# Two of four groups of the inverse products moved into the state chain, on four 64x64 tiles of the array

## What is computed

```python
def step(S, inp):
    rt, wt, kt, vt, at, bt = inp
    sa = jnp.einsum('dbhvk,dbhk->dbhv', S, at)
    S = S * wt[..., None, :] + sa[..., :, None] * bt[..., None, :] + vt[..., :, None] * kt[..., None, :]
    y = jnp.einsum('dbhvk,dbhk->dbhv', S, rt) if emit else None
    return S, y
```

## Time and profile before

| what | value |
|---|---|
| median of 3 runs | 2757.31 us (2756.01 to 2758.84) |
| the profiled execution, own time | 2753.63 us |
| its span | 2751.8 us |
| PE busy | 2687.9 us (98%) |
| DVE busy | 1404.5 us (51%) |
| ACT busy | 734.9 us (27%) |
| mean granted PE clock | 0.996 |

### The profile page before, as it was taken

How to read it: one execution, slowest core, us unless ns; L and a number is a source line. 1 busy time by engine, 2 the same in 40 slices (tenths; PEclk the granted TensorE clock), 3 DMA queues, 4 the chain that set the end, 5 groups by cost and what they waited for, 6 DMA issues and landing times.

```text
span 2751.8 us, 61051 instructions
## 1 busy us (share of the span) xinstructions
PE 2687.9 (98%) x26901; PEld 1731.7 (63%) x26901; DVE 1404.5 (51%) x2723; ACT 734.9 (27%) x1502; POOL 215.1 (8%) x184
## 2 busy tenths in 40 slices
PE   7999999999999999999999999999999999999999
PEld 3455555556444445748888444666666677788887
DVE  2676666674322233337778212677777633314541
ACT  3234333432222221111111002433443322211110
POOL 1000000000000002215444000000000000000000
PEclk9999999999999999999999999999999999999999
DMA  7111111111333333344543224222221234346554
GB/s 266 55 51 43 51 43 51 51 41 43 107 100 105 97 112 92 92 131 148 154 129 107 71 76 141 61 59 59 59 59 51 58 109 111 110 139 191 153 148 121
DMA packets 500007, 264.52 MB, mean 96 GB/s; under 512 B 42864, under 2 KB 493888, under 8 KB 499232
## 3 DMA queue, kind: packets, MB, share of 16 engines
q1 hardware_dynamic: 498016, 251.58, 31.7%
q0 software_dynamic: 1728, 9.03, 0.9%
HBM read 255.33 MB, written 5.24 MB: 95 GB/s over the span
## 4 chain that ended last, share of the span: by engine, by line
PE 91%; ACT 5%; DVE 2%; issue 1%; DMA 1%; SPq 0%; ACTq 0%; DVEq 0%
PE psum L515 34%; PE psum L517 14%; PE psum L1181 12%; PE psum L1293 8%; PE psum L781 2%; PE psum L549 2%; PE psum L1014 1%; PE psum L890 1%; PE psum L1002 1%; PE psum L590 1%; PE psum L992 1%; PE psum L758 1%; PE psum L731 1%; PE psum L771 1%; PE psum L904 1%
## 5 line engine op out<-in xcount | busy, mean ns | idle before, releaser
L515 PE MATMUL psum<-hT,strips 128*128 128x256 f32 (+1 forms) x2252 | 706.4, 464 | 0.8 <-issue 0.8
L515 PEld LDWEIGHTS psum<-hT,strips 128*128 128x128 f32 x2252 | 418.7, 191 | 228.4 <-issue 191.7
L517 PE MATMUL psum<-hT,strips 128*64 128x512 f32 (+1 forms) x1896 | 393.5, 535 | 2.1 <-DVE arena L2372 1.4
L1293 PE MATMUL psum<-arena,strips 128*128 128x512 f32 (+1 forms) x704 | 227.6, 486 | 0.6 <-DVE arena L2811 0.6
L1293 PEld LDWEIGHTS psum<-arena,strips 128*128 128x128 f32 x704 | 133.7, 190 | 93.1 <-issue 83.2
L517 PEld LDWEIGHTS psum<-hT,strips 128*64 128x64 f32 x1896 | 116.5, 136 | 108.0 <-issue 84.5
L515 PE MATMUL psum<-arena,strips 128*128 128x256 f32 (+1 forms) x416 | 125.9, 461 | 0.9 <-DVE done L2660 0.9
L2811 DVE SCALAR_TENSOR_TENSOR arena<-psum,mod,arena 128x256 f32<-128x256 f32 x24 | 10.9, 481 | 193.7 <-PE psum L1293 193.7
L515 PEld LDWEIGHTS psum<-arena,strips 128*128 128x128 f32 x416 | 78.9, 190 | 45.0 <-issue 36.8
L2193 DVE TENSOR_SCALAR arena<-arena 128x512 f32<-128x512 f32 (+1 forms) x88 | 70.0, 795 | 70.1 <-ACT arena L2045 68.0
L1181 PE MATMUL psum<-arena,rwkv_branch 128*128 128x256 f32 x424 | 99.0, 379 | 0.0
(11 more groups left out here) (303 smaller groups left out, 4169.0 us busy)
## 6 DMA issues: line engine op xcount, KB each, us to landing
strips<-in_w_in_dram SPq DMA_DIRECT2D x152, 512.0 KB, 3.8
strips<-in_ada_w_dram SPq DMA_DIRECT2D x80, 512.0 KB, 4.9
strips<-in_ffn_up_dram SPq DMA_DIRECT2D x46, 512.0 KB, 3.8
strips<-in_ffn_down_dram SPq DMA_DIRECT2D x32, 512.0 KB, 3.8
conv_branch<-in_ffn_up_dram SPq DMA_DIRECT2D x28, 512.0 KB, 4.9
arena<-in_ada_w_dram SPq DMA_DIRECT2D x4, 2048.0 KB, 15.9
strips<-in_w_in_dram SPq DMA_DIRECT2D x32, 256.0 KB, 3.3
strips<-in_a_out_w_dram SPq DMA_DIRECT2D x16, 512.0 KB, 3.8
```

The source lines that it names most:

```text
L515: return pe.matmul(o, lhs, rhs, start=start, stop=stop, skip_group_check=True)
L517: ins = pe.matmul(o[64 * h:64 * h + 64], lhs[:, 64 * h:64 * h + 64], rhs, start=start, stop=stop, skip_group_check=True)
L1293: ins = mm(s.o[:, lo:T], strip[:, b, j, :], hid[:, k, lo:T], k == 0, k == FT - 1)
```

## The change

`through_inverse` is called three times for a group: once ahead of the chain for m = 0 and 1, once behind `state_in(1)` for m = 2, and once behind `state_in(2)` for m = 3. The late two go into a Q buffer instead of an A buffer. There the products of row half p write bank p, and head h = 1 writes the other half of the partitions, so that the four (p, h) fall on four different 64x64 tiles; ACT copies them out with four copies of half the length. The dense steps between m = 1 and m = 2 in layer 0 go; instead 4 units (layer 0) or 3 (layer 1) follow m = 1, halved; the hops are a little smaller. `diagonal_blocks(i + 1)` moves ahead of the last hop. In layer 1 the pair products of the context chunks (64 columns) are issued as two 64x64 products each. On ACT `values(0)` or, in layer 0, `conv_gate(i + 1)` goes ahead of the late copies. On DVE `keys(0)` is one chunk earlier in the last group of layer 0. SP waits until ada units 0 and 1 have landed before it issues units 2 and 3.

```diff
@@ pair_products
                     for c in range(4 * j, 4 * j + 4):
-                        for h in range(2):
+                        for e in range(2 if n == CH else 0):
+                            for h in range(2):
+                                ins = one(PS[rows(e), b0 + h, (c % 4) * n:(c % 4 + 1) * n], BK[d][rows(h), c, e, :],
+                                         ar[d][rows(h), c, 0, :])
+                        for h in range(2 if n == P else 0):
                             ins = one(PS[:, b0 + h, (c % 4) * n:(c % 4 + 1) * n],
@@ through_inverse on PE
-                def through_inverse(i, ahead, steps):
-
-                    for j in range(2):
-                        pe.wait_ge(*slots[f"v{j}", l, i].freed)
-                    pe.wait_ge(*slots["t10", l, i].freed)
-                    sv = take(Q, "mv", l, i)
-                    for m in range(4):
-                        if m == 2 and ahead and wide:
-                            fill(steps, 2)
-                        s = take(A, f"lrb{m}", l, i)
+                def through_inverse(i, ahead, first):
+
+                    if first == 0:
+                        for j in range(2):
+                            pe.wait_ge(*slots[f"v{j}", l, i].freed)
+                        pe.wait_ge(*slots["t10", l, i].freed)
+                        sv = take(Q, "mv", l, i)
+                    for m in range(2) if first == 0 else (first,):
+                        s = take(A if m < 2 else Q, f"lrb{m}", l, i)
...
-                                ins = one(PS[r, BANK_A[s.b], q * n:(q + 1) * n].rearrange("p (k t) -> p k t", t=CH),
+                                to = rows(p if m < 2 or h == 0 else 1 - p)
+                                bank = BANK_A[s.b] if m < 2 else BANK_P[s.b] + p
+                                ins = one(PS[to, bank, q * n:(q + 1) * n].rearrange("p (k t) -> p k t", t=CH),
@@ the group on PE
-                    through_inverse(i, ahead, steps)
-                    hop = (3.4 if ahead else 4) if wide else 2 if ahead else 2.3
+                    through_inverse(i, ahead, 0)
+                    halved[0] = True
+                    fill(steps, 4 if wide else 3)
+                    hop = (3.3 if ahead else 4) if wide else 1.8 if ahead else 2.1
                     for c in range(NCH):
                         state_in(c, i)
-                        halved[0] = True
+                        if c in (1, 2):
+                            through_inverse(i, ahead, c + 1)
                         if c == NCH - 1:
                             outputs_of_states(i)
+                            if ahead:
+                                diagonal_blocks(i + 1)
                         if c > 0:
                             fill(steps, hop)
                         if c < NCH - 1:
                             state_out(c, i)
                             fill(steps, hop)
-                    if ahead:
-                        diagonal_blocks(i + 1)
                     fill(steps, everything)
@@ SP
                     if l == 0 and c == COL_W:
+                        for u in range(2):
+                            sp.wait_ge(adab.full[u], 16)
                         load_unit(512)
                         load_unit(D + 512)
@@ ACT
-                def through_inverse(i):
-                    for m in range(4):
+                def through_inverse(i, m0, m1):
+                    for m in range(m0, m1):
                         s = filled(f"lrb{m}", i)
+                        if m > 1:
+                            for p in range(2):
+                                o = PS[:, BANK_P[s.b] + p, :].rearrange("p (d h k t) -> p d h k t", d=2, h=2, k=2)
+                                for h in range(2):
+                                    r, at_ = (slice(64 * x, 64 * x + 64) for x in (p, p if h == 0 else 1 - p))
+                                    ins = act.copy(EE[r, 1:3, 1, :, h, 2 * (m % 2) + p].rearrange("p k d t -> p d k t"),
+                                                   o[at_, :, h])
+                            ins.then_inc(s.free, 1)
+                            continue
...
-                    through_inverse(i)
+                    through_inverse(i, 0, 2)
+                    if not ahead:
+                        values(0)
+                    elif lo == 0:
+                        conv_gate(i + 1)
+                    through_inverse(i, 2, 4)
                     if ahead:
-                        if lo == 0:
-                            conv_gate(i + 1)
                         conv_centre(i + 1)
...
                     else:
-                        values(0)
                         values(1)
@@ DVE
-                        if not ahead and c == (4 if lo else 3):
+                        if not ahead and c == (4 if lo else 2):
                             keys(0)
```

More of the change, by code:

```diff
@@ L1782, in through_inverse @@
                         ins.then_inc(s.free, 1)
-                        if m < 2:
-                            value_products(m, i)
+                        value_products(m, i)
                 def conv_gate(i):
```

## The result

| | kernel before | changed kernel |
|---|---|---|
| median | 2758.06 us (2756.01 to 2758.84, 4 runs) | 2731.23 us (2729.31 to 2734.66, 4 runs) |
| profiled execution, own time | 2753.63 us | 2730.94 us |
| its span | 2751.8 us | 2729.1 us |

The ratio is 0.9903, with a 95% interval of 0.9892 to 0.9915: faster by 1.0%, or 22.7 us between the two profiled executions, where I had written 21.8. By the medians it is 26.8 us here, and 24.3 us when both kernels were measured again (first experiment). The total hides misses of opposite sign, so here is where PE stands in the two traces, read as the start of the same product in each.

A forecast was written before the change was run, and what follows sets the result against it. PE, busy 2687.9 of 2751.8 us, was taken as the bound. Layer 0 (-6.9, last group -2.0), layer 1 (-9.6, last -2.3) and start (-1.0) sum to -21.8 us: 2731.8 profiled, 2735.5 median; range 2724 to 2750.

The forecast's parts named there:

- The late products: `through_inverse`, m = 2 and 3: 70 to 35 ns a record on four tiles; -1.13 us (layer 0), -1.46 (layer 1) a group.
- first rival: Late products: the four tiles don't overlap, 70 ns a record stays, +4 us, 2761; chance 0.10.
- Switches: Changes of tile shape on PE, some 0.1 us each: -0.15 and -0.1 us a group in layer 0, -0.1 in layer 1.
- the +0.1 that never came: Layer 0's chain at chunks 1 and 4, fitting by under 0.1 us: +0.1 us in each of 7 groups.
- Stalls in the hops: PE waits on DVE: `gated` +0.3 us in layer 0; before `state_out(3)` and `state_in(6)` +1.05 in layer 1, each of 7 groups.
- the rival by which they do not show (2726): Hops: extra cover lets DVE catch up, waits stay under 0.2 us a group, -9 us; chance 0.17.
- the one by which layer 1's chain absorbs the gain (2749): Layer 1: each of 7 groups stalls 2 us more because DVE is nearly full, +14 us; chance 0.10.
- The pair products: Layer 1's context chunks: 32 split records take 0.56 us at 17.5 ns each; -0.86 us in each of 8 groups.
- The last group of layer 0: The 1.1 us wait for `keys(0)` goes, the second V strip waits 0.2 more: -0.9 us, -2.0 with late products.
- The start: The second ada unit lands earlier, as units 2 and 3 no longer share the DMA engines: -1.0 us of 0 to 1.7.
- the other side: ACT's late copies are slower than taken and hold the chain through 32 waits: +20 us, 2777; chance 0.05.
- The rest of layer 1: Layer 1's 8 chains: -1.37 us in each of 7 groups, -2.3 in the last, -11.9 in all.

The follow-up runs named there:

- first experiment: The changed kernel unedited, measured again beside the kernel before: 2732.07 us, ratio 0.9912, against 2756.32 us.
- two-tile run: Changed kernel with the late products still in the chain, but both heads writing the partitions of their own row half: 2745.03 us, ratio 0.9959.
- run with the earlier frees: Changed kernel with `gated` and `keys(1)` one chunk earlier on DVE and layer 1's hop 2 instead of 1.8: 2722.22 us, ratio 0.9876.
- run ahead of the chain: Changed kernel with the four-tile late products and ACT's copies issued right behind the early ones: 2775.81 us, ratio 1.007.
- doubled products: Layer 1's first-group context pair products whole, issued twice: 2731.58 us in the changed kernel (split kept in other groups), 2755.55 us in the kernel before.

## Why the prediction was right, and where it was not

**The late products** were the main term and right. I took 0.56 us for 16 records and the trace has 0.55; 70 ns a record became 34. The two-tile run holds the other half of it: 13 us is what four tiles give over two, so the first rival (the tiles don't overlap, 2761) is out. In layer 1 the late products mix with `state_in` in the trace; at 0.55 us each as in layer 0 they cost 1.43 us less a group (1.01 work, 0.42 waits), forecast 1.46.

**Switches** were mis-sized. A layer 0 group went from 74.71 to 73.23 us, -1.48 instead of -0.98. The late products follow `state_in` in the same tile shape, and each time `state_in` costs 0.17 instead of 0.27 us, and about as much less in layer 1 (0.82 us with the late products, where 0.37 and 0.55 would be 0.92): -0.2 a group in both layers, a term that my own 0.1 us a switch would have given had I applied it there. With the dense steps (-0.3, forecast -0.25) and the +0.1 that never came, this is most of the 3 us of layer 0.

**Stalls in the hops** were right, each in place and nearly in size: 0.60 us of waiting for `gated` (forecast 0.6, up from 0.37 instead of 0.33), 0.53 before `state_out(3)` (0.6), 0.28 before `state_in(6)` (0.4). The run with the earlier frees took them away and gained 9.9 us, so the rival by which they do not show (2726) is out, and so is the one by which layer 1's chain absorbs the gain (2749): there are no waits in chunks 3 to 7 beyond these two.

**The pair products** gave 0.60 us a group, forecast 0.86. A split set costs 0.69 us (1745.20 to 1746.15, less the wait of 0.26), 22 ns a record, not 17.5; and the next piece then waits 0.26 us for DVE (L2498), so 0.34 is left. My row of 11 ns (128 records of 32 columns on sixteenths) was too kind a guide. The rule in the page "TensorEngine Tiling (Array Packing)" of the Trainium skill, section Instruction Overhead, about 60 cycles a product, gave an estimate of 25 ns and 0.8 us for a set; the trace lies between it and me, a little nearer to it. The page says of up to 60 columns that they take the same time, not of every size, as I had put it; these products have 64. By its own work the split gives under 3 us; the rest of what the run without it lost is the first group's gaps and clock, less what the later groups' gaps gave back.

**The last group of layer 0** is a step that failed. I wrote that its 1.1 us wait "should go with its earlier place", naming `keys(0)`. It did not go; it grew from 1.10 to 2.03 us, since what PE needs there is the buffer that `keys(1)` frees at c = 5, and PE now gets there sooner. -0.9 forecast, +0.9 measured. Moving `keys(1)` took it away. The group as a whole still gained 1.7 us of the 2.0 forecast, since its late products with their waits went from 2.96 (670.75 to 673.71) to 1.10 us.

**The start** is the other step that failed: 0 instead of -1.0 us. I had the second unit land earlier because units 2 and 3 no longer share the DMA engines with it. Its products do start 0.95 us earlier (22.72 after, 23.67 in the earlier trace rows), but 0.93 of that is there before PE uses any unit (the wait for x ends at 9.99 instead of 10.91); the wait for the unit is 1.64 us instead of 1.70. New is a wait of 1.6 us for a strip, and the first `half_step` waits for DVE, 3.1 us instead of 2.5. I took only PE's waits for the unit and not what ends last behind them.

The pair of traces is kind to the edit, too: the first `half_step` starts at 120.93 before and at 120.97 after, but at 121.0 to 124.8 us (mean 123.1) in the nine traces with SP's wait, and at 120.2 to 121.4 (mean 120.9) in the five without it. All nine have a wait of 1.2 to 2.9 us for that strip, four of the five without have at most 0.5 (the fifth 1.9); and in the five that start at 123.8 or later the granted clock falls to 0.50 behind it, near 39 us (this row and window are the changed kernel's, measured again):

```profile
39.19 2.53 PE L549 MATMUL psum<-hT,strips 128*128 128x512 f32 x3 [2.59 <-DMA strips<-in_w_in_dram]
```

```profile
39.50:43.00 3.50, 3.50 (x5) 0.51 1.05 365
```

So by the traces the wait costs some 2 us at that point rather than giving 1; the medians of the two runs without it are too close to confirm or deny that.

**ACT** (the other side, 2777) held nothing up: 1.50 us against my 1.46. The run ahead of the chain shows that this rival was not idle talk, since there PE's waits for ACT are 30.8 us.

**The first group of layer 1** was in no term but for its pair products, and is worth 7.3 us of the 22.7: most of it a gap of 3.61 us and the half clock behind it. The doubled products show that these do not hang on work or tiles, and the packets tie them to blocks of instructions. Without this group I was 6 us too optimistic. The rest of layer 1 gave 6.9 instead of 11.9: a group without "issue" gaps gained 1.1 instead of 1.37 us, and the next six groups together only 4.1. Their "issue" gaps did not shrink (8.3 us before, 8.4 after, at other pieces and up to 3.9 us a group), and behind one of 1.62 us that ends at 1980.90 the changed kernel runs at half the clock for some 3.4 us, where the kernel before stays at 1.00 from 1777 to 2200 (windows of the changed kernel, then of the kernel before):

```profile
1981.00:1984.50 3.50, 3.50 (x18) 0.51 0.02 5
```

```profile
1777.00:2200.00 423.00, 411.22 (x8158) 1.00 0.21 58
```

That the sum came out within a microsecond of the profiled execution is therefore largely luck: 7.3 us that I had not seen and 3.0 more than forecast in layer 0 stand against 5.0 less in the rest of layer 1, 1.0 at the start and 3.4 between and behind the layers.

One sum of the prediction is wrong: in the first rival 0.3 x 8 is 2.4, not 2.7. It moves that rival by 0.3 us and nothing else.

What stays open: the times between layers (+2.0) and at the end (+1.4) differ between the two profiles of the kernel before by 1.3 and 1.4 us, with other places where the clock falls, and I didn't follow them.

## What to carry to other kernels

Small products with half the array idle double their rate when they are spread over all four quadrants, but only if they lie where their evacuation has time: the same products a few microseconds earlier made the kernel slower. Walk the dense steps over each hop, since the three stalls in the hops were readable from rows of the trace before; and before a wait is called gone, find which operation frees the very buffer. A gain in a place where no work changed is a sign to look at gaps without a releaser: compare them with the instruction queue's packets and with the granted clock behind them before the edit gets the credit. One pair of traces does not price an edit of 1 us at the start: the same program got there up to 3.8 us later in another execution.

## What the runs showed that I had not expected

- Waits for instructions: gaps of PE without a releaser, up to 3.73 us, end 2.2 to 2.9 us behind a packet of 16.4 KB on the instruction queue (39 of 39 gaps above 0.8 us). They were 13.1 us in seven groups of layer 1 of the kernel before, and they move when instructions are added: doubling 16 products took 9.8 us away in one kernel and nothing in another.
- The price of a gap is more than the gap: behind 3.61 us of standing still the granted clock was 0.50 for 7 us (3.4 us more), and behind a wait of 2.38 us it fell in four groups of layer 0 and stayed at 1.00 in three others.
- 64x64 products with 128 columns: on two tiles into one bank 70 ns a record for 32 in a row and 64 for 16, on two tiles into two banks 61 for 16, on four tiles into two banks 34 for 16.
